# First phase of a two-block transformer kernel: x turned once and raw, scaled before it is normed, with GpSimd norming it for later chunks

## The reference, cut to what matters

```python
def modulate(h, shift, scale):
    return h * (1 + scale[:, None, :]) + shift[:, None, :]

def hybrid_layer(x, c_act, w_ada, b_ada, w_in, ...):
    mod = c_act @ w_ada + b_ada                 # 1024 x 6144, six sections
    shift_mix, scale_mix, gate_mix, shift_ffn, scale_ffn, gate_ffn = jnp.split(mod, N_MOD, axis=-1)
    h = modulate(rms_norm(x), shift_mix, scale_mix)
    proj = h @ w_in                             # qa, ka, va, qb, kb, vb
    ...
def memory_attention(q_mem, mem, mem_norm, w_mem_kv):     # second block, prepared early
    kv = rmsnorm(mem, mem_norm) @ w_mem_kv
    ...
```

## Time and profile before

| | |
|---|---|
| median of 3 runs | 1804.58 us (1804.25 to 1805.24) |
| profiled execution, time | 1805.17 us |
| profiled execution, span | 1803.5 us |
| PE busy | 1771.0 us, 98% of the span |
| DVE busy | 1094.9 us, 61% |
| ACT busy | 732.6 us, 41% |
| POOL busy | 40.4 us, 2% |
| granted TensorE clock, mean | 0.997 of full speed |

### The profile page before, as it was taken

The page is one execution under the profiler, slowest core; times in us unless marked ns, Lnnn a source line. Parts: engine busy times, 40 slices in busy tenths (PEclk is TensorE's granted clock), DMA queues, the critical chain, the costliest instruction groups (busy, mean ns, idle before and its releaser), DMA issues.

```text
span 1803.5 us, 22462 instructions
## 1 busy us (share of the span) xinstructions
PE 1771.0 (98%) x8312; PEld 1430.2 (79%) x8312; DVE 1094.9 (61%) x1601; ACT 732.6 (41%) x1031; POOL 40.4 (2%) x78
## 2 busy tenths in 40 slices
PE   7999899999999999999999999999999999999998
PEld 6887556888888888878888888889766888888887
DVE  6978775655555335775677765245577567677423
ACT  7313664343334323444444443233365434444322
POOL 4110000000000000000000000000000000000000
PEclk9999999999999999999999999999999999999999
DMA  9794112223322233312332222323401232222231
GB/s 358 249 341 139 48 53 94 82 94 103 105 93 87 91 102 94 110 55 93 103 106 94 93 93 82 111 83 101 175 24 47 73 115 93 93 93 93 95 104 70
DMA packets 149081, 195.29 MB, mean 108 GB/s; under 512 B 3646, under 2 KB 133000, under 8 KB 146332
## 3 DMA queue, kind: packets, MB, share of 16 engines
q1 hardware_dynamic: 141272, 155.28, 26.5%
q0 software_dynamic: 7600, 39.13, 5.8%
q10 hardware_dynamic: 148, 0.05, 0.0%
HBM read 189.15 MB, written 5.29 MB: 108 GB/s over the span
## 4 chain that ended last, share of the span: by engine, by line
PE 94%; DVE 4%; ACT 1%; issue 1%; DMA 0%; SPq 0%; ACTq 0%; DVEq 0%
PE bank L809 21%; PE bank L810 21%; PE bank L811 21%; PE bank L872 3%; PE bank L874 3%; PE bank L873 3%; PE bank L1478 2%; PE bank L1479 2%; PE bank L1480 2%; PE bank L956 2%; PE bank L1141 1%; PE bank L1008 1%; PE bank L852 1%; PE bank L853 1%; PE bank L854 1%; PE bank L977 1%
## 5 line engine op out<-in xcount | busy, mean ns | idle before, releaser
L1949 DVE TENSOR_TENSOR w_lo<-w_stage,w_hi 128x2048 fp32r<-128x2048 f32 (+3 forms) x135 | 296.6, 2197 | 436.6 <-ACT w_hi L1506 436.4
L809 PE MATMUL bank<-act_hi,w_hi 128*128 128x512 f32 x1216 | 475.2, 391 | 0.9 <-DVE act_lo L2013 0.6
L811 PE MATMUL bank<-act_hi,w_lo 128*128 128x512 f32 x1216 | 473.2, 389 | 0.0
L810 PE MATMUL bank<-act_lo,w_hi 128*128 128x512 f32 x1216 | 473.1, 389 | 0.0
L1506 ACT ACTIVATE w_hi<-w_stage 128x2048 fp32r<-128x2048 f32 (+3 forms) x137 | 251.7, 1837 | 461.5 <-PE bank L811 334.0
L809 PEld LDWEIGHTS bank<-act_hi,w_hi 128*128 128x128 f32 x1216 | 228.2, 188 | 50.6 <-DVE act_lo L2013 2.1
L810 PEld LDWEIGHTS bank<-act_lo,w_hi 128*128 128x128 f32 x1216 | 228.3, 188 | 47.5 <-issue 0.5
L811 PEld LDWEIGHTS bank<-act_hi,w_lo 128*128 128x128 f32 x1216 | 228.2, 188 | 47.3
L809 PE MATMUL bank<-mid_hi,w_hi 128*128 128x512 f32 x352 | 136.9, 389 | 0.0
L810 PE MATMUL bank<-mid_lo,w_hi 128*128 128x512 f32 x352 | 136.9, 389 | 0.0
L811 PE MATMUL bank<-mid_hi,w_lo 128*128 128x512 f32 x352 | 136.9, 389 | 0.0
(11 more groups left out here) (412 smaller groups left out, 2630.2 us busy)
## 6 DMA issues: line engine op xcount, KB each, us to landing
ada_stage<-in_w_ada POOLq DMA_DIRECT2D x24, 1024.0 KB, 7.2
w_stage<-in_w_up SPq DMA_DIRECT2D x22, 1024.0 KB, 5.1
w_stage<-in_a_ffn_in SPq DMA_DIRECT2D x22, 1024.0 KB, 5.0
w_stage<-in_b_ffn_in SPq DMA_DIRECT2D x22, 1024.0 KB, 5.1
w_stage<-in_w_in SPq DMA_DIRECT2D x10, 1024.0 KB, 7.3
w_stage<-in_b_ffn_out SPq DMA_DIRECT2D x10, 1024.0 KB, 5.0
w_stage<-in_w_down SPq DMA_DIRECT2D x8, 1024.0 KB, 5.2
w_stage<-in_a_ffn_out SPq DMA_DIRECT2D x8, 1024.0 KB, 5.1
```

Of the source, the lines that this page charges most:

```text
L809: pe.matmul(dst, wh, mh, start=start and k == 0, stop=False)
L810: pe.matmul(dst, wh, ml, start=False, stop=False)
L811: last = pe.matmul(dst, wl, mh, start=False, stop=stop and k == nk - 1)
L1949: dve.tensor_tensor(w_lo[slot][:, 0:n], raw[:, 0:n], w_hi[slot][:, 0:n].bitcast(FP32), ALU.subtract).then_inc(w_ready, 1)
```

## The change

x is turned once, raw, into `x` at the very start, among the turns of `mem` and the products of `mem_half(0, ...)`. The query chunks 0 and 1 take `x` times scale without the norm. The norm of a token is a factor of a column of their output, so it is applied when the output is copied out of PSUM (`norm_tile(dst, src, rms, ...)`). For this the inverse root of each token is spread over all partitions: four products of `neg_ones` with `diag` into a bank, copied by ACT to `rms` with factor -1. GpSimd multiplies `x` by `rms` into `x_norm`, 8 instructions of 128x512, for chunk 2 and later. The squares of x are shared: two tiles of tokens on ACT, two on DVE. The sum of the modulation for SCALE_MIX is made by eight products with a column of ones, one output column each, in place of eight turns and a sum along the row. The weights of chunk 0 are split in two halves, and its two output tiles are summed side by side, tile of x by tile of x. The small loads of the convolutions go to a new place (`conv_rows`) and are issued behind the GpSimd products; the load of `rel_bias` ahead of them.

```diff
@@ gpsimd
+            pool.dma_start(rb_rows[:, :], a["rel_bias"][0]).then_inc(rb_loaded, 16)
+            pool.wait_ge(rms_row, 1)
+            for k in range(KT):
+                pool.tensor_tensor(x_norm[:, k, :], x[:, k, :], rms[:, :], ALU.mult).then_inc(x_normed, 1)
             small_loads()
@@ tensor
-            pe.wait_ge(x_diag, NT)
-            for k in range(KT):
...
-                for t in range(NT):
-                    last = scaled_turn(bank[4 + k % 4], x_tok[:, t, P * k:P * (k + 1)], t)
-                last.then_inc(xn_turned, 1)
...
-            mem_half(0, 0, range(4))
...
-            ada_sum(range(8, 16), 2)
-            mem_half(0, 0, range(4, KT))
-            mem_half(0, 1)
+            def scale_sum():
+
+                pe.wait_ge(consts_set, 14)
+                pe.wait_ge(ada_added, 8)
+                pe.wait_ge(x_saved, KT)
+                for j in range(8):
+                    last = pe.matmul(bank[2][:, j:j + 1], ada_acc[:, P * (8 + j):P * (9 + j)], one_col,
+                                     start=True, stop=True)
+                last.then_inc(mod_summed, 1)
+
+            for k in range(KT):
+                turn_mem(k)
+                if k >= 4:
+                    turn_x(k - 4)
+            for k in range(KT):
+                pe.wait_ge(tr_saved, TR0["mem"] + k + 1)
...
+                if k == KT - 1:
+                    scale_sum()
+                for m in range(2):
+                    mem_half(0, m, [k])
+                if k < 4:
+                    turn_x(4 + k)
+            pe.wait_ge(x_diag, NT)
+            for t in range(NT):
+                last = pe.matmul(bank[3][:, P * t:P * (t + 1)], neg_ones[:, :], diag[:, t, :], start=True,
+                                 stop=True)
+            last.then_inc(rms_spread, 1)
...
+            pe.wait_ge(w_half, 2)
+            for k in range(KT):
+                if k == KT // 2:
+                    pe.wait_ge(w_ready, 1)
+                for m in range(2):
+                    part(C0["qk_a"], 0, m, [k], act, tile_wait=normed("w_in_scaled") if m == 0 else None,
+                         start=k == 0, stop=k == KT - 1)
...
-                if j == 1:
-                    pe.wait_ge(mem_saved, 1)
-                    turn_x(range(4))
...
-                    turn_x(range(4, 8))
@@ scalar
+                if k >= 4:
+                    save_x(k - 4)
+            act.wait_ge(x_loaded, 16)
+            for k in range(4, KT):
+                save_x(k)
+                if k in (4, 6):
+                    t = k // 2 - 2
+                    act.activation(sq_junk[2 + t][:, :], x_tok[:, t, :], ACT.Square,
+                                   accum_out=x_ss[:, t:t + 1]).then_inc(x_squared, 1)
...
+            act.wait_ge(w_loaded[0], 16)
+            first_half(0)
             act.wait_ge(scaled, SPLIT0["w_in_scaled"] + 8)
             for t in range(KT):
-                act.activation(act_hi[:, t, :], x_norm[:, t, :], ACT.Copy, scale=modv(SCALE_MIX, t))\
+                act.activation(act_hi[:, t, :], x[:, t, :], ACT.Copy, scale=modv(SCALE_MIX, t))\
                     .then_inc(act_hi_done, 1)
+                if t == 2:
+                    first_half(1)
+                    act.wait_ge(rms_spread, 1)
+                    act.activation(rms[:, :], bank[3][:, :], ACT.Copy, scale=-1.0).then_inc(rms_row, 1)
             split_at(1)
             for t in range(KT):
-                act.wait_ge(act_ready, t + 1)
+                act.wait_ge(x_normed, t + 1)
                 act.activation(x_norm[:, t, :], x_norm[:, t, :], ACT.Copy, scale=modv(SCALE_MIX, t))\
                     .then_inc(scaled, 1)
@@ vector
-                    if j < 2:
+                    if ph == "qk_a" and j < 2:
+                        last = norm_tile(dst, src, rms, HD ** -0.5)
+                    elif j < 2:
                         last = dve.tensor_scalar(dst, src, HD ** -0.5, None, ALU.mult)
...
+            dve.wait_ge(c_act, 1)
+            for n in range(4):
+                ada_first(n)
             dve.wait_ge(x_root, 1)
             dve.reciprocal(x_rms, x_rms).then_inc(x_inv, 1)
...
             dve.wait_ge(mod_summed, 1)
-            dve.tensor_reduce(out=mod[:, 8:16], in_=banks[:, 2:4, :].rearrange("p b (c n) -> p (b c) n", n=P),
-                              axis=AXIS.X, op=ALU.add).then_inc(mod_added, 1)
-            dve.wait_ge(mod_added, 1)
-            dve.scalar_tensor_tensor(out=mod[:, 8:16], in0=mod[:, 8:16], scalar=1.0, in1=vec[:, P + 8:P + 16],
+            dve.scalar_tensor_tensor(out=mod[:, 8:16], in0=bank[2][:, 0:8], scalar=1.0, in1=vec[:, P + 8:P + 16],
                                      op0=ALU.add, op1=ALU.add).then_inc(scaled, 8)
-            split_w(0, 0)
...
             for t in range(KT):
+                if t == 3:
+                    first_split(1)
                 low_scaled(t)
```

More of the change, by code:

```diff
@@ L1729, in _, with first_half @@
                 last.then_inc(tr_saved, 1)
-            for k in range(KT):
-                act.wait_ge(xn_turned, k + 1)
-                act.activation(x_norm[:, k, :], bank[4 + k % 4][:, :], ACT.Copy).then_inc(xn_saved, 1)
-            def save_x(tiles):
-                for k in tiles:
-                    act.wait_ge(x_turned, k + 1)
-                    act.activation(x[:, k, :], bank[4 + k % 4][:, :], ACT.Copy).then_inc(x_saved, 1)
-            split_at(0)
+                if k >= 4:
+                    save_x(k - 4)
[6 more added lines that the diff above has]
+                                   accum_out=x_ss[:, t:t + 1]).then_inc(x_squared, 1)
+            act.wait_ge(x_squared, NT)
+            act.activation(x_rms, x_ss, ACT.Sqrt, scale=1.0 / D, bias=eps).then_inc(x_root, 1)
+            def first_half(half):
+                part = slice(1024 * half, 1024 * half + 1024)
+                act.activation(w_hi[0][:, part], w_stage[0][:, part], ACT.Copy)\
+                    .then_inc(w_hi_done if half else w_half, 1)
+            act.wait_ge(w_loaded[0], 16)
+            first_half(0)
             act.wait_ge(scaled, SPLIT0["w_in_scaled"] + 8)
             for t in range(KT):
-                act.activation(act_hi[:, t, :], x_norm[:, t, :], ACT.Copy, scale=modv(SCALE_MIX, t))\
+                act.activation(act_hi[:, t, :], x[:, t, :], ACT.Copy, scale=modv(SCALE_MIX, t))\
                     .then_inc(act_hi_done, 1)
+                if t == 2:
+                    first_half(1)
+                    act.wait_ge(rms_spread, 1)
+                    act.activation(rms[:, :], bank[3][:, :], ACT.Copy, scale=-1.0).then_inc(rms_row, 1)
             split_at(1)
             for t in range(KT):
-                act.wait_ge(act_ready, t + 1)
+                act.wait_ge(x_normed, t + 1)
                 act.activation(x_norm[:, t, :], x_norm[:, t, :], ACT.Copy, scale=modv(SCALE_MIX, t))\
@@ L1758, in _ @@
                                        bias=modv(SHIFT_MIX, t)).then_inc(act_hi_done, 1)
-                    save_x(range(4))
-                if j == 2:
-                    save_x(range(4, 8))
             def rel_splits(t):
@@ L2250, in _ @@
             dve.wait_ge(x_loaded, 16)
-            for t in range(NT):
-                if t:
-                    dve.wait_ge(x_squared, t)
-                dve.tensor_tensor_reduce(out=x_junk, in0=x_tok[:, t, :], in1=x_tok[:, t, :], scale=1.0,
+            for t in range(2, NT):
+                dve.tensor_tensor_reduce(out=sq_junk[2 + t][:, :], in0=x_tok[:, t, :], in1=x_tok[:, t, :], scale=1.0,
                                          scalar=0.0, op0=ALU.mult, op1=ALU.add,
```

86 lines of the change are left out of this document (40 added, 46 removed).

## The result

The changed kernel takes **1810.22 us** (median of 8 runs, 1808.91 to 1812.09), the kernel before 1803.88 us (8 runs, 1803.08 to 1805.24): a ratio of 1.0036, 95% interval 1.0027 to 1.0045. It is slower by 6.3 us, and 0.2 above the upper end of the predicted range (1810.0). The profiled execution took 1812.09 us with a span of 1810.4 us, 6.9 more than before.

What follows compares the result with a forecast made beforehand. PE's chain of waits was taken as the bound, DVE only about 0.65 us from it. -4.7 without GpSimd, +0.8 clock and +4.6 GpSimd gave +0.7 on 1804.6: 1805.3 us, range 1800.2 to 1810.0, about 8 in 10.

Steps and rivals of the forecast that it cites:

- the sum: Whole kernel: -4.7 without GpSimd, +0.8 for the clock, +4.6 for GpSimd, together +0.7 us.
- the clock's price: Ahead of chunk 2, PE's wait may lower its granted clock: 0 to 1.7 us, taken as +0.8.
- Between bounds this far apart I take a bit over half, +4.6: DVE's loss beside GpSimd's eight products, landing on chunk 2: bounds 0 and 8.6 us, taken as +4.6.
- the second rival: DVE waits for each GpSimd instruction in full: +8.6, 1809.3 us, or 1810.2 with the full clock price; chance 0.28.
- its forecast (2 to 7): DVE loses 2 to 7 us beside GpSimd's products: 1802.5 to 1807.5 us; chance 0.36.
- DVE got by the short ones unharmed: DVE's squares kept their pace beside GpSimd's short selections, a reason to take +4.6 below the bound of 8.6.
- so I take 1.7: Before `scaled`: the eight one-column products take 1.7 us on PE; the reduction of 1.23 goes.
- at about 28.5: Before `scaled`: PE's and ACT's new lists end at about 28.5, half a microsecond either way open.
- chunk 0 no earlier than 35: Start of chunk 0: a sign that the prediction is wrong in place; it expected a start near 33.
- The second batch, -1.75: Raw turns of x behind chunk 3, on the chain with nothing beside them: dropping them takes 1.75 us off.
- Behind 90 us I see no new bound: After the part that the change touches, the first 90 us, nothing new was expected to limit the kernel.
- the first rival: GpSimd costs DVE under 1 us: -3.9, 1800.7 us, or 1799.9 with a clock that holds; chance 0.28.

Runs made afterwards that it cites:

- experiment 1: The changed kernel without the eight GpSimd products, ACT scaling raw x in their place; 1802.34 us, ratio 0.9988 to the kernel before.
- Experiment 5: The changed kernel with GpSimd's eight products reading x alone (x times 1.0) in place of x and `rms`; 1804.23 us, one run.
- experiment 2: The changed kernel with filler matmuls on PE, ten ahead of the scale's sum and sixteen ahead of the shift's turns; 1807.9 us, ratio 1.0019.
- experiment 10: The changed kernel with the shift's eight turns behind chunk 1's last matmul instead of ahead of its last nine; 1809.05 us, ratio 1.0030.
- experiment 9: The kernel before with early raw turns alone, none behind chunk 3, normed turns kept, buffers moved, no GpSimd products; 1802.86 us, ratio 0.9990.
- experiments 3: The changed kernel without GpSimd products and with PE fillers, ten ahead of the scale's sum and eight behind chunk 1; 1803.51 us, ratio 0.9995.

## Why the prediction was wrong

The sign of the sum was right, which at +0.7 says little, and its sizes weren't. Without GpSimd the sum was -3.9 with the clock's price; experiment 1 measured -2.0. Point by point:

- **"Between bounds this far apart I take a bit over half, +4.6"** is the term that failed most: it measured 7.1 (experiment 1), 0.89 for each product. The mechanism is that of the second rival, nearly in full; its bound of 8.6 was a fifth too high. A loss of 7.1 lies between what the prediction gave its forecast (2 to 7) and what it asked of that rival (7.5). My reason for less, that "DVE got by the short ones unharmed", looked at instructions of another size and kind: selections of 128 columns with one operand. Experiment 5 shows 0.35 us on a DVE instruction for one operand of 512 columns, against 1.04 for the two of the change; a quarter of 0.35 hardly shows in a square of 1.23 (in the second trace of the changed kernel one beside a selection took 1.34). The row spoke of a form that the change doesn't use. The Trainium skill's rule (SBUF, State Buffer, "Who interferes with whom") gives that second rival, and for two operands the trace agrees: 7.1 us lost. For one operand it agrees too, at a smaller price: `act_lo` takes 1.10 us in place of 0.74 where the two meet.
- **"so I take 1.7"** for the one-column products, and `scaled` at 30.6: 3.04 us and 32.0. At full clock they take 1.84 and `scaled` comes at 31.0 to 31.2, so 0.4 to 0.6 us of the miss of 1.4 stay at full clock, 0.14 of it the size; the rest is the clock. Behind it lies the count that PE's list ends "at about 28.5": it ended at 26.6, and PE stood still for 2.24 us.
- **The clock, "+0.8"**, was placed ahead of chunk 2 alone. It fell in two places, at 28 to 36 and at 60 to 68, and costs about 2.8 us (experiment 2). The sign that the prediction named, "chunk 0 no earlier than 35", is this: 35.16.
- **A wait that the sum didn't have**: the shift's turns stand ahead of the last nine matmuls of chunk 1, and they wait for the partial sums and for DVE's copy of chunk 0 (`group_free`). As long as PE was the later chain this cost nothing. With DVE late, PE stands 4.18 us, the nine matmuls end at 67.3, and `act_hi` starts 1.85 us behind the shift, where it was 0.7 before. The second rival said that PE would stand there, and gave it no price. By itself the order can't be shown to cost time, since the clock takes its gain (experiment 10).
- **The second batch, -1.75**, held in the main: 1.4 in the trace of experiment 9, 1.0 in its medians.
- **"Behind 90 us I see no new bound"** held, as far as the rows reach, but experiments 3 and 9 found one ahead: DVE waits 2.07 and 1.47 us for chunk 2's weights. With chunk 2 at 60.0 in place of 61.24, and 1.75 us off, that makes about 1801.6 from the prediction's 1804.6 (an estimate), and not the first rival's 1799.9.
- **The second rival's 1810.2** with the full clock price is the measured time to a tenth, and that is luck: it has 8.6 for GpSimd, a start 3.05 us early that never came, 1804.6 for the kernel before in place of 1803.88, and no price for PE's wait.

The sum as it was, for chunk 2's start: `scaled` -1.0, ACT's wait +0.4, GpSimd +7.1, the copy +0.1, `act_hi` held +1.2; together +7.8, which is 69.02 - 61.24. The prediction had -2.5, 0, +4.6, +0.1 and -0.65 in these places and +0.8 for the clock, together +2.35. Less 1.75 for the second batch it is 6.0, and the first matmul of the values' chunks starts 6.1 us later than before (91.97 against 85.83). The spans differ by 6.9, the medians by 6.3; the rest lies spread behind 92 us, within what single runs of a kernel differ by, and isn't assigned.

## What to carry to other kernels

Work handed to GpSimd isn't free when it reads tiles beside a DVE that never pauses: price it as if the busy engine did it, and compare with really doing it there (5.38 us against 7.1 here). When the chain changes engines, look again at every instruction that was placed for the old one; a wait in the middle of a chunk costs nothing until its engine is the early one. Ask when the next weights land before pricing a gain: a chain can only come forward as far as its data. A gain ahead of a stretch of PE work can come back as a lower clock, so look what PE does in the time won.

## What the runs showed of the hardware

- GpSimd's product of two 128x512 operands beside DVE takes 1.36 to 3.33 us, DVE's `act_lo` beside it 1.78 to 1.79 in place of 0.74 (the first one 1.34). Filling the same tile takes 0.53 and costs DVE nothing.
- What one GpSimd instruction of 128x512 adds to the DVE instruction that it holds up: 1.02 to 1.04 us with two operands, 0.77 with two reads of one tile, 0.35 with one operand, nothing when it only writes. DVE's copies out of PSUM keep their 0.74 beside it. GpSimd's recorded length (medians 1.74, 1.48, 1.70) includes its own wait and says little of this.
- A one-column matmul isn't cheap: 0.115 us a pass at the 2.4 GHz level (1.84 for 16), 0.19 to 0.22 near 1.2 GHz. A turn of 128 columns takes 1.06/8 = 0.13 by the same rows.
